# A decoder layer with expert retrieval: products and gates of the dense stage read for eight tiles at a time

## What is computed

```
q = h @ w_q                                  # 8 heads, two halves of 128
top 16 of the sums of the two halves' scores -> 16 experts and 16 gates for each head and token
act[t, k] = gelu(u[expert[t, k]] . h[t]) * gate[t, k]
out[t] = x[t] + sum over k of act[t, k] * v[expert[t, k]]
```

## Time and profile before

| | |
|---|---|
| Median of 3 runs | 2954.48 us |
| The profiled execution's own time | 2953.46 us |
| Its span in the profile | 2951.7 us |
| TensorE busy | 2885.2 us (98%) |
| VectorE busy | 2356.0 us (80%) |
| GpSimd busy | 1540.0 us (52%) |
| ScalarE busy | 1054.8 us (36%) |
| DMA | 980.65 MB, mean 332 GB/s |
| DMA in the last quarter of the span | 401 to 419 GB/s |

### The profile page before, as it was taken

The page is one execution under the profiler, slowest core; times in us unless marked ns, Lnnn a source line. Parts: engine busy times, 40 slices in busy tenths (PEclk is TensorE's granted clock), DMA queues, the critical chain, the costliest instruction groups (busy, mean ns, idle before and its releaser), DMA issues.

```text
span 2951.7 us, 40402 instructions
## 1 busy us (share of the span) xinstructions
PE 2885.2 (98%) x14993; PEld 2566.0 (87%) x14993; DVE 2356.0 (80%) x3050; ACT 1054.8 (36%) x1375; POOL 1540.0 (52%) x906
## 2 busy tenths in 40 slices
PE   7999999999999999999999999999999999999998
PEld 6888777788899999999999999999997777777776
DVE  6455677755678888988888898899777999898998
ACT  4122343341333333434333343334233333333332
POOL 1000232300006766665756666577867878877852
PEclk9999999999999999999999999999999999999999
DMA  8998777779758998999999899999999999999998
GB/s 302 328 353 276 252 240 247 227 295 316 242 177 310 347 334 302 341 322 336 316 319 333 304 336 323 337 336 365 333 352 401 413 416 412 417 418 418 419 417 357
DMA packets 324223, 980.65 MB, mean 332 GB/s; under 512 B 62756, under 2 KB 179504, under 8 KB 240752
## 3 DMA queue, kind: packets, MB, share of 16 engines
q1 hardware_dynamic: 179488, 508.60, 46.4%
q0 software_dynamic: 107008, 439.75, 41.4%
q10 hardware_dynamic: 37584, 30.43, 3.2%
HBM read 866.33 MB, written 112.33 MB: 332 GB/s over the span
## 4 chain that ended last, share of the span: by engine, by line
PE 68%; DVE 13%; DMA 10%; issue 5%; ACT 2%; POOL 1%; ACTq 0%; DVEq 0%; SPq 0%; POOLq 0%
PE ps L1863 21%; PE ps L1865 21%; PE ps L1864 21%; DMA v_two<-in_peer_v 9%; PE ps L2104 3%; DVE x_rows L1713 2%; DVE v_lo L1762 2%; ACT v_hi L1216 2%; DVE u_row L1704 1%; DVE x_one L1811 1%; DVE uT_lo L1672 1%; DMA v_ring<-in_peer_v,experts 1%; DVE uT_lo L1677 1%; PE ps L1946 1%; PE ps L1962 1%
## 5 line engine op out<-in xcount | busy, mean ns | idle before, releaser
L1863 PE MATMUL ps<-hT_hi,uT_hi 128*128 128x384 f32 x2048 | 698.5, 341 | 5.1 <-DVE uT_lo L1672 2.3
L1865 PE MATMUL ps<-h2T_lo,uT_hi 128*128 128x384 f32 x2048 | 686.1, 335 | 0.0
L1864 PE MATMUL ps<-hT_hi,uT_lo 128*128 128x384 f32 x2048 | 684.9, 334 | 0.0
L852 POOL DMA_INDIRECT gate_grid<-gates,grid_cells x256 | 533.7, 2085 | 105.8 <-issue 78.6
L1863 PE MATMUL ps<-v_hi,a_hi 128*128 128x512 f32 x1024 | 403.5, 394 | 34.9 <-DVE v_lo L1762 34.2
L1216 ACT ACTIVATE v_hi<-v_two 128x2048 fp32r<-128x2048 f32 x126 | 241.4, 1919 | 445.9 <-PE ps L1865 306.1
L1864 PE MATMUL ps<-v_hi,a_lo 128*128 128x512 f32 x1024 | 400.5, 391 | 0.0
L1865 PE MATMUL ps<-v_lo,a_hi 128*128 128x512 f32 x1024 | 400.3, 391 | 0.0
L1863 PEld LDWEIGHTS ps<-hT_hi,uT_hi 128*128 128x128 f32 x2048 | 384.8, 188 | 13.5 <-DVE uT_lo L1677 6.6
L1864 PEld LDWEIGHTS ps<-hT_hi,uT_lo 128*128 128x128 f32 x2048 | 385.0, 188 | 1.9
L1865 PEld LDWEIGHTS ps<-h2T_lo,uT_hi 128*128 128x128 f32 x2048 | 384.4, 188 | 0.0
(11 more groups left out here) (209 smaller groups left out, 4975.8 us busy)
## 6 DMA issues: line engine op xcount, KB each, us to landing
v_two<-in_peer_v SPq DMA_DIRECT2D x63, 2048.0 KB, 11.8
u_tile<-in_peer_u SPq DMA_DIRECT2D x72, 1024.0 KB
u_tile<-uT_all SPq DMA_DIRECT2D x56, 1024.0 KB
near_rows<-in_peer_u SPq DMA_DIRECT2D x40, 1024.0 KB, 8.1
uT_all<-near_turned SPq DMA_DIRECT2D x100, 256.0 KB, 7.0
w_raw<-in_w_in SPq DMA_DIRECT2D x24, 1024.0 KB, 9.2
wc_raw<-in_w_in SPq DMA_DIRECT2D x48, 512.0 KB, 6.6
far_rows<-in_peer_u SPq DMA_DIRECT2D x16, 1024.0 KB, 9.2
```

Of the source, the lines that this page charges most:

```text
L852: pool.indirect_dma_start(out=gate_grid, out_offset=bass.IndirectOffsetOnAxis(ap=grid_cells[:, d, col:col + 1], axis=0), in_=gates[:, 2 + ...
L1863: mm(out, a_hi, b_hi, start=first, stop=False)
L1864: mm(out, a_lo, b_hi, start=False, stop=False)
L1865: return mm(out, a_hi, b_lo, start=False, stop=last)
```

## The change

Groups 0 and 1 (tiles 0 to 7) stay as they are. From tile 8 on, products and gates come for eight tiles at a time ("a wide", four pairs), as two DMAs of 1 MB with runs of 8 KB, into two buffers of 8 KB per partition for each of them. A partition then holds the experts `8 p` to `8 p + 7` of a wide's 1024, and the loads of `v` follow this order: two tiles and 16 KB runs as before, but 64 KB from partition to partition. Wide 1 is loaded at tile 1 after the v load there, wide 2 at tile 5, and from then on a wide at every eighth tile (5, 13, 21 and so on, the last, wide 15, at tile 109). Each load waits for the last rest of the buffer's earlier use. The new buffers lie over memory that is free by then; `x_end` moves, and three late arrays are placed earlier in their arena.

```diff
+WIDE = 2 * GROUP
+SMALL_GROUPS = 2
+WIDE_LATE = 5.5
+WIDE_PAIRS = WIDE // 2
...
-        x_end = [at(f"x_end{i}", kb, [P, D]) for i, kb in enumerate((72, 136))]
+        x_end = [at(f"x_end{i}", kb, [P, D]) for i, kb in enumerate((72, 184 + WIDE_LATE))]
+        wide_dots = [at(f"wide_dots{i}", kb, [P, WIDE, GRID]) for i, kb in enumerate((104, 72))]
+        wide_gates = [at(f"wide_gates{i}", kb, [P, WIDE, GRID]) for i, kb in enumerate((136, 184 + WIDE_LATE))]
...
-        def pair_of(groups, pair):
-            half = pair % (GROUP // 2)
-            return groups[pair // (GROUP // 2) % GROUP_RING][:, 2 * half:2 * half + 2, :]
+        def wide_ring(wide):
+            return (wide - 1) % GROUP_RING
+        def pair_of(small, wide, pair, first):
+            if first and pair < WIDE_PAIRS:
+                half = pair % (GROUP // 2)
+                return small[pair // (GROUP // 2)][:, 2 * half:2 * half + 2, :]
+            part = pair % WIDE_PAIRS
+            return wide[wide_ring(pair // WIDE_PAIRS)][:, 2 * part:2 * part + 2, :]
...
-            def load_two(group, half):
-                sp.dma_start(v_two[half][:, :, :], v_rows(group)[:, 2 * half:2 * half + 2, :]).then_inc(v_two_in[half], 16)
+            def load_two(wide, pair, first):
+                if first and pair < WIDE_PAIRS:
+                    rows = v_rows(pair // 2)[:, 2 * (pair % 2):2 * (pair % 2) + 2, :]
+                else:
+                    part = pair % WIDE_PAIRS
+                    rows = v_table[bass.ds(wide * WIDE * P, WIDE * P), :]\
+                        .rearrange("(p j) d -> p j d", j=WIDE)[:, 2 * part:2 * part + 2, :]
+                sp.dma_start(v_two[pair % 2][:, :, :], rows).then_inc(v_two_in[pair % 2], 16)
...
+            def load_wide(ring, wide):
+                rows = bass.ds(wide * WIDE * P, WIDE * P)
+                sp.dma_start(wide_dots[ring][:, :, :].rearrange("p j t -> p (j t)"),
+                             products_dense[rows, :].rearrange("(p j) t -> p (j t)", j=WIDE)).then_inc(group_in[ring], 16)
+                sp.dma_start(wide_gates[ring][:, :, :].rearrange("p j t -> p (j t)"),
+                             grid_v[rows, :].rearrange("(p j) t -> p (j t)", j=WIDE)).then_inc(group_in[ring], 16)
...
             def dense(h, first=False, last=False):
                 for b in range(TOPK):
-                    group = TOPK // GROUP * h + b // GROUP
+                    wide = TOPK // WIDE * h
                     if b % 2 == 1 and not (last and b + GROUP >= TOPK):
                         sp.wait_ge(v_lo_ready, TOPK * h + b + 1)
                         if first and b == 1:
                             for n in range(2):
                                 sp.wait_ge(v0_used[n], TILES // 2)
-                        load_two(group + 1, b // 2 % 2)
-                    if b % GROUP == 1 and not (last and b // GROUP + GROUP_RING >= TOPK // GROUP):
+                        load_two(wide + (b // 2 + 2) // WIDE_PAIRS, b // 2 + 2, first)
+                    if first and b == 1:
+                        sp.wait_ge(a_lo_ready, 2)
+                        load_wide(wide_ring(1), 1)
+                    if b % WIDE == 5 and not last:
                         sp.wait_ge(a_lo_ready, TOPK // 2 * h + b // 2 + 2)
-                        load_group(b // GROUP % GROUP_RING, group + GROUP_RING)
+                        load_wide((b // WIDE + 1) % GROUP_RING, wide + b // WIDE + SMALL_GROUPS)
...
-            sp.wait_ge(v0_used[0], TILES // 2)
-            sp.wait_ge(v0_used[1], TILES // 2)
+            sp.wait_ge(a_lo_ready, TILES // 2 - WIDE_PAIRS)
             for d in range(DENSE):
                 sp.dma_start(x_end[d][:, :], x_mid[1 + d]).then_inc(x_in[2 + d], 16)
...
             def weigh_pair(pair):
-                dve.wait_ge(group_in[pair // 2 % GROUP_RING], 32 * (pair // 2 // GROUP_RING + 1))
-                v.tensor_tensor(pair_of(dots_at, pair), pair_of(dots_at, pair), pair_of(gates_of, pair), ALU.mult)\
+                if pair < WIDE_PAIRS:
+                    dve.wait_ge(group_in[pair // 2], 32)
+                else:
+                    wide = pair // WIDE_PAIRS
+                    dve.wait_ge(group_in[wide_ring(wide)], 32 * ((wide - 1) // GROUP_RING + 2))
+                products_of_pair = pair_of(dots_at, wide_dots, pair, True)
+                v.tensor_tensor(products_of_pair, products_of_pair, pair_of(gates_of, wide_gates, pair, True), ALU.mult)\
                     .then_inc(weights_ready, 1)
```

More of the change, by code:

```diff
@@ L304, in decoder_layer @@
         o_ss = sb("o_ss", [P, TB])
+        experts = late_sb("experts", [P, TB, PEER_HEADS * TOPK], U32)
+        gates = late_sb("gates", [P, TB, PEER_HEADS * TOPK])
+        cells = late_sb("cells", [P, PEER_HEADS * TOPK], U32)
         rest = late_sb("rest", [P, N_KEYS])
@@ L322, in decoder_layer @@
         gate_inv = sb("gate_inv", [P, TB])
-        experts = late_sb("experts", [P, TB, PEER_HEADS * TOPK], U32)
-        gates = late_sb("gates", [P, TB, PEER_HEADS * TOPK])
-        cells = late_sb("cells", [P, PEER_HEADS * TOPK], U32)
         gates_of = [at("gates_of0", 180, [P, GROUP, GRID]), late_sb("gates_of1", [P, GROUP, GRID])]
@@ L716, in _ @@
                 sp.wait_ge(uT_half1_ps[b], turned_by_pe(b, TILES))
-            load_two(0, 1)
+            load_two(0, 1, first=True)
             for b in range(2):
@@ L1193, in sweep @@
                     if last and b == TOPK - 2:
-                        split_pair(0, 0)
+                        split_pair(0, 0, first=True)
                     if more and not first:
@@ L1216, in split_v, with split_pair @@
                 nc.scalar.activation(v_hi[b % 2][:, :], v_raw(h, b), ACT.Copy).then_inc(v_hi_ready, 1)
-            def split_pair(pair, i):
+            def split_pair(pair, i, first=False):
                 act.wait_ge(weights_ready, pair + 1)
-                nc.scalar.activation(a_hi[i % 2][:, :, :], pair_of(dots_at, i), ACT.Copy).then_inc(a_hi_ready, 1)
+                nc.scalar.activation(a_hi[i % 2][:, :, :], pair_of(dots_at, wide_dots, i, first), ACT.Copy)\
+                    .then_inc(a_hi_ready, 1)
             split_u(0, 0, 0)
@@ L1243, in dense @@
                         act.wait_ge(u_used[1], TILES // 2)
-                        split_pair(1, 1)
+                        split_pair(1, 1, first=True)
                         gelu0(TILES - 1)
                     if ahead and b % 2 == 1 and not (first and b == 1):
-                        split_pair(pair + 1, (b // 2 + 1) % 4)
+                        split_pair(pair + 1, b // 2 + 1, first)
             dense(0, first=True, last=False)
@@ L1771, in rest_pair @@
                 dve.wait_ge(a_hi_ready, pair + 1)
-                v.tensor_tensor(a_lo[pair % 2][:, :, :], pair_of(dots_at, pair), a_hi[pair % 2][:, :, :].bitcast(F32),
+                v.tensor_tensor(a_lo[pair % 2][:, :, :], pair_of(dots_at, wide_dots, pair, True), a_hi[pair % 2][:, :, :].bitcast(F32),
                                 ALU.subtract).then_inc(a_lo_ready, 1)
```

## The result

The changed kernel takes 2963.59 us (median of 6 runs, 2962.63 to 2965.72) against 2954.85 us (6 runs, 2951.82 to 2957.42): ratio 1.0033, 95% interval [1.0023, 1.0044]. It is slower by 8.7 us. The forecast was no change at 2951.7 us, and its range ended at 2962.

A forecast was written before the change was run, and what follows sets the result against it. The DMA engines were taken to set the dense stage's pace. Packets -3.4, start -1.9, waits 0, tail +2.5, burst 0 gave -2.8 us on 2953.46: 2950.7, as a median 2951.7 us; range 2945 to 2962.

The forecast's parts named there:

- What bounds the kernel: Dense stage: the DMA engines set the pace, 5.83 us of work per tile against TensorE's 5.44.
- The packets: Product and gate loads: 7680 packets of 4 KB become 3840 of 8 KB, saving 3.4 us, at best 5.6.
- rival C: Loads of v: reads slow with the 64 KB partition step, v packets pass 0.63 us; 2961 us, chance 0.03.
- The start and the tail: Start: extra megabyte fills idle DMA time in 2219 to 2236, -1.9 us; last 18 tiles: engines idle more, +2.5 us.
- The added waits: SyncE's added or moved waits, for buffer reuse, and later landings of weights: cost nothing, 0 us.
- The burst: 2 MB wide load before a v load: queued gathers go ahead, pace stays, 0 us; far ends +27 and -17.
- rival A: Each wide load: late v stops TensorE over 3 us, fewer gathers issue, queue 0 runs dry; 2964 us, chance 0.18.
- Rival B: Dense stage: queue 1 gets half the bandwidth, v tiles come in time, gathers take the debt; -7.8, 2946.7 us, chance 0.22.

The follow-up runs named there:

- e12: The changed kernel with gathers kept 6 ahead of their addition instead of 8, the ring's memory unchanged; 2969.63 us.
- e3: The kernel before (4 KB runs, 32 KB step, its tile order) with two groups, 2 MB, loaded at once every eighth tile; 2994.40 us.
- e11: The changed kernel without GpSimd's fetches of single products for heads 1 to 7 (output differs); 2982.34 us.
- e1: The changed kernel with a wide's products loaded four tiles after its gates, so 1 MB before a v load instead of 2 MB; 2949.44 us.
- e10: The kernel before without the loads of the gates of groups 2 to 31 (output differs); 2930.93 us.
- e2: The changed kernel's tile order and 64 KB step, but half-wide loads with 4 KB runs at the kernel before's places; 2955.77 us.
- e4: The changed kernel with TensorE multiplying zeros six times before its wait for tiles 26, 42, 58, 74, 90 and 106; 2960.91 us.
- e5: The changed kernel with each wide load cut by partition halves into four 512 KB DMAs, one behind each v load; 3072.52 us.

## Why the prediction was wrong

**What bounds the kernel: right.** From the kernel before to the changed one it is +9.4 us idle and +8.7 us time; to e12 +14.5 and +14.8; to e3 +35.2 and +39.5; to e11, which has less work, +35.4 and +27.5. Idle time alone does not order the table: e1 is faster than the kernel before with 0.7 us more of it, as its two queues are busy 701.1 us of the stage and not 706.3. The stage's length is work plus idle time by the way that these are taken, so the sums are no proof by themselves; that the engines set the pace is shown by e10, which takes work away and falls by 23.9 us.

**The packets: right in size, not to be seen in the sum.** Packet by packet (2300 to 2850 us), 8 KB on queue 1 last 0.316 us in the changed kernel against 2 x 0.167 in the kernel before. Without the burst the runs bring 6.4 us (e1 against e2), more than the 3.4 taken and a little over the upper end of 5.6; where the rest comes from is not shown. In the changed kernel the v packets last 0.634 us against 0.623 in the kernel before (0.617 in the prediction, which reckoned from the queue's share), past the 0.63 that was to point at rival C. But in e1, with the same 64 KB step, they last 0.623, and in e3, with the 32 KB step and the burst, 0.638. So it goes with the burst and not with the step, and what lengthens them is open.

**The start and the tail: right.** The share is 1.00 for 0.89 in 2219 to 2236. `v_hi` does not wait for v in the last 13 tiles, and over the last 100 us of the stage the share is 0.91 against 0.93, 2 us more idle where 2.5 were taken. No run measured either by itself; together with the runs, all that is not the burst gives 5.4 us (e1 against the kernel before), where the sum had 2.8. **The added waits: right,** none of them shows.

**The burst: this step failed.** Its term in the sum was 0, and it measured 14.2 us (the changed kernel against e1). It said: "as long as gathers are queued, a late v tile only lets them go ahead, and the pace stays at the work per tile. So I take 0". The size of the stop was foreseen ("at most 1.3 + 3.1 = 4.4"; the longest wait of TensorE is 4.7). In the changed kernel SyncE issues a v load, a wide, and 11 us later the next v load,

```profile
2422.14 0.33 SPq L686 DMA_DIRECT2D v_two<-in_peer_v  x1
2422.78 0.33 SPq L699 DMA_DIRECT2D wide_dots<-products_dense  x1
2423.21 0.38 SPq L701 DMA_DIRECT2D wide_gates<-gate_grid  x1
2433.20 0.33 SPq L686 DMA_DIRECT2D v_two<-in_peer_v  x1
```

ScalarE can use that last one only at 2449.99, 16.8 us after its issue (start, duration, in brackets the wait),

```profile
2449.99 3.71 ACT L1246 ACTIVATE v_hi<-v_two 128x2048 fp32r<-128x2048 f32 x2 [8.10 <-DMA v_two<-in_peer_v]
```

and TensorE starts tile 42 after a wait of 4.06 us, its first matmul at twice the usual duration:

```profile
2449.91 0.39 PE L1901 MATMUL ps<-v_lo,a_hi 128*128 128x512 f32 x1
2454.36 0.79 PE L1899 MATMUL ps<-v_hi,a_hi 128*128 128x512 f32 x1 [4.06 <-DVE v_lo L1793]
```

What failed is the premise that queue 0 always has gathers to go ahead with. While the v load waits behind the wide, the gathers keep half of the engines (52.4% in 2435 to 2443), and the five issued from 2439 on land ever sooner, 18.1, 12.3, 9.9, 9.7 and 6.9 us after their issue: nothing is left standing in the queue. Then the v load issued at 2459.46 has landed (8.8 us later), queue 1 is empty until the next is issued at 2472.76, and queue 0 has next to nothing left. Below are queue 0 and queue 1 in 2467 to 2470 us, then in 2470 to 2474 with the DMA engines' busy tenths in 40 slices of 0.1 us, and last what GpSimd issues:

```profile
q0 software_dynamic: 216, 1.12, 98.9%
q1 hardware_dynamic: 6, 0.00, 0.1%
```

```profile
DMA  9695595595797799792020000000000000000999
q0 software_dynamic: 140, 0.75, 45.9%
q1 hardware_dynamic: 14, 0.23, 26.0%
```

```profile
2465.77 2.19 POOL L901 DMA_INDIRECT v_ring<-in_peer_v,experts  x1 [0.30 <-issue]
2468.27 2.56 POOL L890 DMA_INDIRECT dots<-products_one,cells  x1 [0.30 <-issue]
2471.14 2.27 POOL L890 DMA_INDIRECT dots<-products_one,cells  x1 [0.30 <-issue]
2473.71 2.56 POOL L901 DMA_INDIRECT v_ring<-in_peer_v,experts  x1 [0.30 <-issue]
```

For some 1.6 us (16 slices in a row at 0) the DMA engines do next to nothing. GpSimd is not waiting for a ring place here: it issues a gather and two fetches in turn, one gather in 6.9 us (five rounds from 2439.39 to 2473.71), while the 1 MB of a gather is an estimated 2.5 us of work for the engines at 417 GB/s. The same holds for the seven clearest stretches of idle engines before the last 200 us (2312 to 2315, 2400 to 2402, 2471 to 2475, 2564.5 to 2567, 2662 to 2665, 2741 to 2743 and 2752.5 to 2755): GpSimd is busy 16.8 of their 19 us, and it waits for `x_one` in none of them. Two of them, columns as in rows 1:

```profile
2471.00:2475.00 4.00, 4.00 (x20) 3.30 (x19) 4.00 (x3) 1.13 (x1) 3.56 (x2) 1.00 0.58 182
...
2662.00:2665.00 3.00, 2.29 (x10) 1.91 (x11) 3.00 (x3) 1.72 (x1) 2.69 (x2) 1.00 0.60 172
```

So where the changed kernel idles, GpSimd's pace is what binds at that moment, with no queued gathers to cover it. How many are queued is bounded by the 8 places: with two fewer the engines idle 5 us more (e12), and with GpSimd quick the places themselves bind (e11, 107 waits), and they idle 26 us more.

The prediction had this as rival A at 0.18, with both limits, the ring and the three issues per row; it set against it that gathers stand in the queue for 17.7 to 31.4 us. Those landings were a sign of the balance of the kernel before, in which v was never late by much, and the change itself did away with it (14.9 us). What a queue holds under one order of transfers is no bound for another. That A's price of 2964 came out is luck in part: it was 14 bursts at 0.7 us, 9.8 us, with no gain elsewhere, and what came is 14.2 us for the bursts less 5.4 for the rest.

**A step that was missing: the clock.** After the stop shown the granted clock is at its lower level (1.2 of 2.4 GHz) for part of the next microseconds (a mean of 0.73 over 8 us), and the matmuls of the stage took 7.3 us more. This looked like the whole loss. By e4 it is worth about 2.7 us, no more than the intervals can tell, since TensorE does not set the pace.

**Rival B** was a picture of another kernel: it is what e1 does. The longest wait for v is 4.8 us, gathers are at times waited for, and it is 5.4 us faster (B gave 7.8).

## What to carry to other kernels

Where the DMA engines are full, a change is worth what it does to their work and to their idle time. Ask, for each queue and each moment, what it could still issue, and by what that is limited (ring places, waits, the pace of the engine that issues), not what it held in the trace of before. Here 8 KB runs were good beside a queue of 8 KB runs (6.4 us); a burst of 2 MB in front of a v load that is wanted soon after its landing was not (14.2 us). Keep the runs and put the two loads apart: that version, at 2949.4 us, beats both kernels.

## What had not been expected of the hardware

- Two queues with 8 KB runs each share the DMA engines packet for packet (145 and 145 in 5 us); with 4 KB against 8 KB it was 150 against 259 GB/s.
- In a transfer of 64 partitions an 8 KB packet lasts 1.71 times as long as in one of 128 (0.541 against 0.316 us), the gathers' packets beside it 1.23 times, while every DMA engine counts as busy (e5).
- Less work on a queue can make a kernel slower: 112 fetches fewer, 18.7 us more (e11).
- The clock's fall to its lower level after such a stop costs little where another resource sets the pace: 9.1 us of matmul time saved, about 2.7 us of time (e4).
